# Seven products instead of eight in one more block of an MLP, its operand differences in a lent part of x, and new numbers in the planner of the order

## The reference

```python
D_MODEL = 1024; SEQ = 2048; DEPTH = 4; MLP_HIDDEN = 4 * D_MODEL

def channel_mlp(h, w1, w2):
    return jnp.square(jax.nn.relu(h @ w1)) @ w2

def reference(x, ...):
    for i in range(DEPTH):
        h = rmsnorm(x, norm_mix[i])
        ...                                    # mixer A, B or C
        x = x + y
        x = x + channel_mlp(rmsnorm(x, norm_mlp[i]), m_w1[i], m_w2[i])
    return rmsnorm(x, norm_final)
```

## Time and profile before

| | |
|---|---|
| median of 3 runs | 3080.59 us |
| profiled execution's own time | 3079.77 us |
| span of its slowest core (core 3) | 3078.2 us |
| spans of the 8 cores | 3070.2 to 3078.2 us |
| PE, DVE, ACT, POOL busy | 98%, 74%, 43%, 24% |
| granted TensorE clock, core 3 | 0.996 |

### The profile page before, as it was taken

How to read it: one execution, slowest core, us unless ns; L and a number is a source line. 1 busy time by engine, 2 the same in 40 slices (tenths; PEclk the granted TensorE clock), 3 DMA queues, 4 the chain that set the end, 5 groups by cost and what they waited for, 6 DMA issues and landing times.

```text
span 3078.2 us, 47408 instructions; the slowest of 8 cores (3070.2 to 3078.2 us)
## 1 busy us (share of the span) xinstructions
PE 3019.1 (98%) x15290; PEld 1439.1 (47%) x15290; DVE 2267.6 (74%) x3775; ACT 1317.5 (43%) x2293; POOL 738.5 (24%) x896
## 2 busy tenths in 40 slices
PE   8999999999999999999999999999999999999998
PEld 3444444444444444444576444444444444444444
DVE  7945767678779987877458788877855757577886
ACT  4312433434655354455534634553322333433554
POOL 1111233101414320132551421212212141201221
PEclk9999999999999999999999999999999999999999
DMA  9699997777867367686422477768897988776674
GB/s 167 109 152 165 165 160 126 164 158 156 165 154 130 62 154 158 150 204 150 104 47 77 100 174 172 166 149 165 140 162 131 160 135 143 155 163 142 153 188 114
DMA packets 137585, 445.45 MB, mean 145 GB/s; under 512 B 12032, under 2 KB 15232, under 8 KB 137344
## 3 DMA queue, kind: packets, MB, share of 16 engines
q0 software_dynamic: 102304, 347.38, 64.4%
q1 hardware_dynamic: 35040, 95.04, 8.7%
HBM read 646.07 MB, written 78.64 MB: 235 GB/s over the span
## 4 chain that ended last, share of the span: by engine, by line
PE 93%; DMA 2%; DVE 2%; issue 1%; ACT 1%; POOL 0%; SPq 0%; DVEq 0%; ACTq 0%; POOLq 0%
PE bank L164 93%; DVE xT L164 1%; DMA xT<-x 1%; DMA x_spill<-xT 1%; DMA ring<-b_w_out 0%; DMA ring<-m_w 0%; DVE m_tv L164 0%; DVE bank L164 0%; DVE hT1v L164 0%; DMA ring<-a_w_in 0%; ACT ring L164 0%; ACT sq L164 0%; ACT rs L164 0%; POOL sacc L164 0%; POOL a_smv L164 0%
## 5 line engine op out<-in xcount | busy, mean ns | idle before, releaser
L164 DVE TENSOR_TENSOR xT<-bank,xT 128x512 f32<-128x512 f32 (+2 forms) x972 | 707.3, 745 | 290.5 <-PE bank L164 270.6
L164 PE MATMUL bank<-m_tv,ring 128*128 128x512 bf16 (+2 forms) x3724 | 814.7, 372 | 11.2 <-DVE xT L164 9.3
L164 PEld LDWEIGHTS bank<-m_tv,ring 128*128 128x128 bf16 x3724 | 358.4, 98 | 434.3 <-issue 24.8
L164 ACT ACTIVATE bank<-bank 128x512 f32<-128x512 f32 x496 | 289.4, 587 | 416.1 <-PE bank L164 340.1
L164 POOL DMA_DIRECT2D ring<-m_w x256 | 137.6, 537 | 1242.4 <-PE bank L164 1189.8
L164 ACT ACTIVATE m_tv<-bank 128x512 bf16<-128x512 f32 x511 | 302.2, 598 | 46.7 <-DVE bank L164 11.2
L164 DVE TENSOR_TENSOR m_tv<-m_tv,m_tv 128x512 bf16<-128x512 bf16 x494 | 221.5, 479 | 97.7 <-ACT m_tv L164 94.9
L164 POOL TENSOR_TENSOR sacc<-sacc,sq 128x512 f32<-128x512 f32 (+1 forms) x162 | 212.0, 1309 | 95.4 <-ACT sq L164 64.0
L164 DVE TENSOR_TENSOR ring<-ring 128x512 bf16<-128x512 bf16 (+1 forms) x384 | 199.9, 537 | 26.7 <-DMA ring<-m_w 18.4
L164 ACT ACTIVATE sq<-xT 128x512 f32<-128x512 f32 (+1 forms) x252 | 152.8, 620 | 144.1 <-POOL sacc L164 91.3
L164 PE MATMUL bank<-m_hv,ring 128*128 128x512 bf16 x704 | 174.6, 379 | 2.2 <-issue 0.3
(11 more groups left out here) (242 smaller groups left out, 4186.5 us busy)
## 6 DMA issues: line engine op xcount, KB each, us to landing
ring<-a_w_in POOLq DMA_DIRECT2D x88, 1024.0 KB, 15.2
ring<-m_w POOLq DMA_DIRECT2D x132, 512.0 KB, 7.1
m_pre<-ring SPq DMA_DIRECT2D x124, 512.0 KB, 6.3
ring<-m_pre POOLq DMA_DIRECT2D x124, 512.0 KB, 7.3
ring<-a_w_out POOLq DMA_DIRECT2D x64, 768.0 KB, 8.5
ring<-m_w POOLq DMA_DIRECT2D x124, 384.0 KB, 6.4
xT<-x SPq DMA_DIRECT2D x16, 512.0 KB, 12.8
ring<-b_w_in POOLq DMA_DIRECT2D x8, 1024.0 KB, 18.7
```

Of the source, the lines that this page charges most:

```text
L164: return lambda e: getattr(e, _method)(*[_r(a) for a in args], **{k: _r(v) for k, v in kwargs.items()})
```

## The change

Pair 0 takes seven products in its last block too (`seven_from` = 3 for all layers). For this:

- `G1` calls `G1s` when `b >= seven_from`; `unit` loads a slab raw and runs `wsums` and `keep` in pair 0.
- `hsums(0, ...)` makes the operand differences of pair 0. S1, m2, n4 lie in the bf16 view of x's tile 3 (channels chunks 0 to 5), two float32 buffers for ACT's copies in chunks 6 and 7. Before that, SP stores tile 3 of x to DRAM (`m_x3`, 2 MB); after the last reader SP loads it back in four pieces. S1, m2 and n4 are made during block 1's turn, m3 in place (over A21 of `mh0`, or `mh2` in layer 2) at the start of block 2's.
- `prep` of tiles 2 and 3 gets three steps a unit instead of one, and is flushed in block 1.
- The table `RELIEFS` replaces `RELIEF` and has the same single entry (1, 3): additions through POOL stay where they were, and none are put into pair 0.
- The planner's numbers change: shorter engine times, longer additions at the end, by engine.

```diff
+    TAIL = {"pe": 0.12, "act": 0.17, "dve": 0.14, "pool": 0.12, "sp": 0.06}
...
-                o.end = s + cost + (0.12 if e == "pe" else 0.06)
+                o.end = s + cost + self.TAIL[e]
...
 def c_act(n=512):
-    return 0.19 + n / 1250.0
+    return 0.08 + n / 1250.0
...
 def c_dve(n=512, mode=1):
-    return 0.155 + n / (960.0 * mode)
+    return 0.08 + n / (960.0 * mode)
...
 def c_pool(n=512):
-    return 0.2 + n / 470.0
+    return 0.15 + n / 480.0
...
     def c_fast(n=512):
-        return 0.18 + n / 1900.0
+        return 0.06 + n / 1900.0
...
+        def unit(kind, p, idx):
+            if p:
+                return load_pre(kind, idx)
+            t, v, vr = load_raw("m_w%d" % (kind + 1), idx)
+            wsums(t, v, vr)
+            keep(kind, idx, t, vr)
+            return four(v), vr
+
         def G1(p, b, i):
-            if p:
+            if p or b >= seven_from:
                 G1s(p, b, i)
                 return
...
+        def hsums(p, which):
...
+            if p:
+                for kc in range(KC):
+                    x_r[kc * NT + 3] = Res(X_OFF + (kc * NT + 3) * 2048, X_OFF + (kc * NT + 4) * 2048)
+                for kc in range(0, KC, 2):
+                    sc.op("sp", I("dma_start", out=xT[:, kc:kc + 2, 1536:2048], in_=m_x3[:, kc:kc + 2, :]), rd=[x3_r],
+                          wr=[xr(kc, 3), xr(kc + 1, 3)], cost=0.06, dma=x3_key[kc // 2], nbytes=128 * 4096, tag="x3", lat=LOAD_LAT)
+            else:
+                sc.op("sp", I("dma_start", out=m_x3, in_=xT[:, :, 1536:2048]), rd=[xr(kc, 3) for kc in range(KC)], wr=[x3_r],
+                      cost=0.06, dma=x3_key[4], nbytes=128 * 16384, tag="x3", lat=LOAD_LAT)
...
         def G1s(p, b, i):
-            w, wr_ = load_pre(0, b * 4 + i)
+            w, wr_ = unit(0, p, b * 4 + i)
...
-            while (p, b) == (0, 2) and work:
-                step()
+            if (p, b + 1) == (0, seven_from):
+                hsums(0, ("m3",))
             for i in range(H_BLK):
                 ahead = more and (i < H_BLK - 1 or turn)
-                if (p, b) == (1, 3):
-                    step(4)
+                step(4 if (p, b) == (1, 3) else 2 if p == 0 else 0)
+                if (p, b + 2, i) == (0, seven_from, 2):
+                    while work:
+                        step()
+                    hsums(0, ("S1", "m2", "n4"))
                 if ahead and (p, b) != (0, 3):
                     G1(*pipe[j + 1], i)
                     if (p, b) == (0, 2) and i == H_BLK - 1:
-                        hsums()
+                        hsums(1, ("S1", "m2", "m3", "n4"))
```

More of the change, by code:

```diff
@@ L540, in build_program @@
         pre_key = [sc.dma_key(f"pre{i}") for i in range(NSLOT)]
+        m_x3 = nc.dram_tensor("m_x3", [128, KC, 512], F32, kind="Internal").ap()
+        x3_r = Res()
+        x3_key = [sc.dma_key(f"mx{i}") for i in range(5)]
         slot_of = lambda t: [q[0] for q in ring].index(t)
@@ L779, in load_raw @@
             last_load[0] = sc.op("pool", I("dma_start", out=t[:, 0:2048], in_=dram[name][l, idx], max_dma_last_dim=8192), wr=[r],
[L780 removed]
+                                 cost=0.55, dma=key, nbytes=512 * 2048, tag="load", lat=LOAD_LAT)
             w_ops.append(last_load[0])
@@ L839, in G1, with hsum @@
             keep(0, b * 4 + i, t_, vr)
-        def hsums():
-            (h0, r0), (h1, r1) = h[3], h[2]
+        SUMS = (("S1", "A21", "A22"), ("m2", "A11", "S1"), ("m3", "A21", "A11"), ("n4", "A12", "m2"))
+        def hsum(p, o, x, y):
+            cut = lambda v: v if p else v.rearrange("p (a b) c -> p a b c", a=2) if len(v.shape) == 3 else v
+            comb(cut(H[o][0]), H[o][1], cut(H[x][0]), H[x][1], cut(H[y][0]), H[y][1], ALU.subtract, 2048)
+        def hsums(p, which):
+            for o, x, y in SUMS if "S1" not in which else ():
+                if o in which:
+                    hsum(p, o, x, y)
+            if "S1" not in which:
+                return
+            H.clear()
+            (h0, r0), (h1, r1) = h[2 * p + 1], h[2 * p]
@@ new lines, in hsums @@
+            for j, k in enumerate(("S1", "m2", "n4")):
+                if p:
+                    t, r = zone("m_h", (128, 4, 512), BF16, h_off + 4 * KB * j)
+                    H[k] = (t[:], r)
+                else:
+                    H[k] = (xb[:, 2 * j:2 * j + 2, 3072:4096].rearrange("p a (b c) -> p a b c", b=2), lent[2 * j:2 * j + 2])
+            H["m3"] = H["A21"]
+            for o, x, y in SUMS:
+                if o in which:
+                    hsum(p, o, x, y)
+            if p:
+                own = [(t[:], r) for t, (r,) in (zone("m_s", (128, 512), F32, h_off + (12 + 2 * j) * KB) for j in range(2))]
+            else:
+                own = [(xs(kc, 3), lent[kc]) for kc in (6, 7)]
@@ L855, in temp @@
+            H["temps"] = own + [(b[0][:], b[2]) for b in sqb]
         def temp():
@@ L864, in prod, with part @@
                 mm = MM if start else MORE
-                sc.op("pe", [mm(bk.v(), w[wk][:, k, :], H[hk][0][:, k, :], start and k == 0, k == 3) for k in range(4)],
+                sc.op("pe", [mm(bk.v(), w[wk][:, k, :], part(H[hk][0], k), start and k == 0, k == 3) for k in range(4)],
                       rd=[wr_[wk]] + H[hk][1], wr=[bk], cost=c_pe(4), tag="W1")
+            def part(v, k):
+                return v[:, k, :] if len(v.shape) == 3 else v[:, k // 2, k % 2, :]
             def copy():
@@ L906, in G2 @@
         def G2(p, b, d):
-            relief = RELIEF if (p, b) == (1, 3) else ()
-            if relief and not xtemp:
+            relief = RELIEFS.get((p, b), ()) if p or not raw_first or b else ()
+            if p and relief and not xtemp:
                 xtemp.extend((t[:], r) for t, (r,) in (zone("m_x", (128, 512), F32, POOL_OFF + (pn[0] % POOL_N + 2 * j) * KB) for j in range(6)))
[L910 to L916, removed]
+            w, wr_ = unit(1, p, b * 4 + d)
             x11, x12, x21, x22 = ((d, 2 * p), (d + 4, 2 * p), (d, 2 * p + 1), (d + 4, 2 * p + 1))
```

28 lines of the change are left out of this document (13 added, 15 removed).

## The result

The changed kernel takes 3101.3 us (median), the one before, measured beside it, 3080.6: ratio 1.0064 with an interval of 1.0051 to 1.0078, 20.7 us slower. The forecast was 3072.6 us, faster, and its range ended at 3085. All times are medians of undisturbed runs (of an even number of runs the upper of the two middle ones; the true median would move a difference by at most 0.7 us). In brackets stand the ratio to the kernel before and its interval.

What follows compares the result with a forecast made beforehand. PE was taken as the bound, 93% of the chain. Terms -13.8 + 5.8 + 2 + 0 - 2 = -8.0 us gave 3072.6 us, 0.26% faster; own range 3067 to 3079, 8-in-10 range 3063 to 3085.

Steps and rivals of the forecast that it cites:

- The rest of the order: Whole program, mainly the joints: new planner intervals gain 2 us; bounds a gain of 8 and a loss of 6.
- Norms moved forward: Blocks 0 and 1: norm steps of tiles 2 and 3 cost nothing, covered by DVE's free 4 us a couple.
- Matmuls removed: Pair 0's last block, four layers: 64 fewer matmuls at 0.216 us, a gain of 13.8 us.
- waits on bank a: New and old seven-product units: PE waits on closely spaced same-bank products, 5.8 us lost; bounds nothing to 8.9.
- DVE in the last block: Pair 0's last block: DVE becomes full, but the lighter block behind catches up; 2 us lost, bounds nothing to 26.
- DVE rival: Turn from block 2 to pair 1: DVE sets the block's end, 4.4 us a layer, total 3088 us; chance 0.14.
- Transfers of x's tile 3: Store and reload by SP in each layer: hidden, cost nothing; other bound 4 x 0.5 us.
- the old seven-product units of pair 1: Sign in pair 1: if these change by more than 4 us in all, the order was the cause, not the products.
- The chance of 0.13 on slower: Whole kernel: probability given to a result slower than before by over 0.2%, 6.2 us.

Runs made afterwards that it cites:

- e9: Changed kernel with DVE's planner numbers put back (one kind of operation, `gate`, also costed differently): -0.4 us against the kernel before, ratio 0.9983.
- e16: Kernel before with all new planner numbers except DVE's (ACT's, POOL's and the tails): -3.4 us, ratio 0.9997.
- e1: Kernel before with all new planner numbers, only the order differing: +27.5 us, ratio 1.0077.
- e5: Kernel before with DVE's new planner numbers alone: +15.1 us, ratio 1.0051.
- e18: e9 with only `c_fast`, the planner's number for sums of two SBUF operands, new: +5.3 us against the kernel before, ratio 1.0051.
- e12: Kernel before with still larger DVE fixed costs in the planner (0.23 and 0.30 us): +46.8 us from two runs, ratio 1.0131.
- e14: e9 with eight products everywhere, nothing lent or transferred, norms still forward: +2.1 us against the kernel before, ratio 1.0007.
- e4: Kernel before with only the norms of tiles 2 and 3 moved forward: +6.2 us, ratio 1.0006.
- e3: Changed kernel with eight products everywhere, nothing lent or transferred; new numbers and forward norms stay: +27.2 us against the kernel before, ratio 1.0075.
- e2: Changed kernel with all old planner numbers, except the cost of one kind of operation (`gate`): +12.9 us against the kernel before, ratio 1.0028.
- e10: Changed kernel with DVE's new numbers only for pair 0's last block and pair 1's first three, old elsewhere: +10.8 us against the kernel before, two runs.
- e15: e9 without the two transfers of x's tile 3, so results are wrong: +6.2 us against the kernel before, from two runs.
- e13: e9 with layer 2 as before (eight products, old norms pace): -4.7 us against the kernel before, ratio 0.9983.

## Why the prediction was wrong, step by step

**The step that failed** is "The rest of the order": "a better order can move little. I take a gain of 2 us; bounds are a gain of 8 ... and a loss of 6". It measured +21.1 us for DVE's numbers within the change (e9), -3.4 for the others on the kernel before (e16), and +27.5 for all of them there (e1). I read true intervals from the trace, saw that the new numbers agreed with them, and took agreement for improvement. DVE's 0.60 us between starts is right, but holds only while nothing disturbs DVE. Over the whole trace of before, a sum of two 512-wide operands has a median of 0.42 us alone (449 `m_tv` and 241 `ring`) and 1.40 and 1.25 us when POOL adds for over half of its length (42 and 13 of them; 11 and 3 stay under 0.6 us). The changed kernel has as many (42 and 16), and all its `m_tv` sums together are stretched by 26.5 us, before by 30.5, so the contention did not grow. The rest is the order: which PE instruction stands behind a late one. That the old numbers' extra 0.08 and 0.12 us work as slack for such lateness fits e5, e9 and e18, but e12 shows that it isn't slack alone, and why `c_dve` weighs more than `c_fast` was not isolated. Shown is: DVE's costs in the planner, this many microseconds, in waits on DVE and in part in clock. Which places in the order make them so costly stays open.

The Trainium skill states the contention ("SBUF — State Buffer", section "Who interferes with whom"): a DVE instruction with two SBUF inputs contends with a GpSimd instruction that reads SBUF. The traces agree, 1.25 to 1.40 us against 0.42. I had not weighed it for either failing step.

**Bounds from busy windows.** I bounded the loss by 6 us because PE was idle for so little before. Idle time bounds what a better order can win, not what a worse one can lose. And a wait was priced at its length; the clock added some 6 us to 19 us of stops. The range was narrower than its own bounds, too: nothing to 8.9 us of bank waits and -8 to +6 us of order around the other terms give 3060.8 to 3083.7, not 3067 to 3079, and with the bounds given for DVE and the transfers the upper end passes 3101.

**Norms moved forward, "cost nothing".** 5.5 to 6.2 us (e14 less e16; e4), in layer 2. I counted DVE's free time as cover and not the POOL additions that move along and stretch it.

**Matmuls removed, waits on bank a, DVE in the last block** (-13.8 + 5.8 + 2 = -6.0). With the new numbers these together measured -6.5. That agreement is luck. In the first pair of layer 1 the changed kernel is 7.3 us shorter than e3, where 16 matmuls fewer can save 3.5, and in the first pair of layer 2 it is 2.3 us longer: the orders differ by more than the products. It is -2.5 with DVE's old numbers and +6.7 with all old ones.

The terms can be read in their own place. I counted PE's matmuls, 240 for pair 0's last block before and 224 now, and took the time from the first to the one behind the last; then the same for the three blocks behind it. Sums over the four layers in us, medians of the six cores whose records have all matmuls:

| kernels | last block of pair 0 | three blocks behind it |
|---|---|---|
| before; changed kernel | 207.2; 198.4 | 590.6; 602.4 |
| new numbers: e3; changed kernel | 207.3; 198.4 | 600.1; 602.4 |
| DVE's old numbers: e14; e9 | 207.2; 198.7 | 591.6; 600.0 |
| all old numbers: e4; e2 | 207.2; 199.3 | 590.7; 609.9 |

In the block itself the forecast was right: 51.81 us before and 49.61 now in each layer (forecast 52 and some 49), or 12.40 a couple, in the forecast's 12.09 to 12.46. The waits there are 49.61 - 224 x 0.216 = 1.2 us a layer, 4.9 in all, for 4.1 forecast. The gain of 7.9 to 8.9 us holds under all three sets of numbers. What the forecast missed is what follows: the blocks behind give back 2.3, 8.4 or 19.2 us. It had given DVE's lateness 2 us in all because "the block behind it is lighter". What PE waits for there was not isolated. The DVE rival's place, the turn, was thus nearer the truth than its size in the changed kernel: DVE reads 43.70 of 48 us in the block (681 to 729 us of layer 0), under the forecast 46 to 48 of 48, and single waits of PE behind it stay at about 2 us or less.

One sign goes against my account of the turn in e10: in e18, with `c_fast` alone new, the first block of pair 1 takes 196.3 us over the four layers against 202.5 in e9, and the loss comes elsewhere, 4.3 us of it in the mixer between layers 0 and 1. A new `c_fast` at the turn alone was not tried.

**Transfers of x's tile 3.** Right by the trace: 21.3 us out, 10.9 us back, and no wait of DVE or PE on them on the slowest core. e15 agrees only in that nothing was gained without them.

The prediction itself said that it would fall if the old seven-product units of pair 1 changed by more than 4 us. The three blocks in the table grew by 11.8 us, of which 9.5 are there in e3 without the new products. So it was in the main the order, not the products. The chance of 0.13 on slower stood, but for 0.01, on one DVE mechanism: apart from a bound of 6 us, a loss by the planner was left out.

## What to carry to other kernels

When a change both removes work and retunes the numbers that lay out the order, take them apart before anything else: here 21 us hung on DVE's costs in the planner, while the 64 products were worth anything from 6.5 us gained to 6.7 lost. A scheduler's cost that agrees with the median of an undisturbed operation is not a better cost; on in-order queues ask what a late operation holds up, and expect slow products behind a stop of several microseconds on TensorE (here 6 us of clock with 19 us of stops). To tell whether removed work paid, time its own stretch and the ones behind it by counted matmuls; a difference of whole runs mixes it with the rest of the order.

The best version is e13 (seven products in layers 0, 1 and 3, DVE's old numbers): 3075.6 us, 0.17% faster than before (0.07 to 0.27%). e16, with no products changed at all, is within 1.3 us of it (its own ratio is 0.9997, 0.9977 to 1.0016), so what the seven products add to it is not shown.

## What the runs showed that was not expected

- The granted clock of single windows of 10 us fell to 0.75 to 0.87 behind stops of 3 to 5 us, in an MLP that otherwise runs at 1.00, and products then lay 0.428 us apart.
- Of the three sets of DVE's fixed costs tried on the kernel before, the middle one is best: `c_dve` at 0.08, 0.155 and 0.23 us (with `c_fast` at 0.06, 0.18 and 0.30) gave +15.1, 0 and +46.8 us.
- Parts of a change to an order don't add: DVE's new numbers cost 15.1 us on the kernel before (e5) and 21.1 in the changed one (e9), and the seven products go from -6.5 to +6.7 us with the numbers around them, though they gain 8 to 9 us in their own block each time.
